# Norms of a two-layer decoder trunk: x turned by products with a diagonal of 1/rms, the upper half of h made by ScalarE from PSUM, lower halves three row blocks later

## The reference

```python
def _rms_norm(x, g):
    y = xf * lax.rsqrt(jnp.mean(xf * xf, axis=-1, keepdims=True) + NORM_EPS)
    return (y * g.astype(jnp.float32)).astype(x.dtype)

def _modulated_norm(x, g, shift, scale):
    return _rms_norm(x, g) * (1.0 + scale[:, None, :]) + shift[:, None, :]

def reference(...):
    for l in range(DEPTH):
        mod = (c_act @ ada_w[l] + ada_b[l]).reshape(bsz, 3, 3, D_MODEL)
        h = _modulated_norm(x, norm_g[l, 0], mod[:, 0, 0], mod[:, 0, 1])
        x = x + MACARON_WEIGHT * mod[:, 0, 2][:, None, :] * _swiglu(h, ffn1_w_in[l], ffn1_w_out[l])
        h = _modulated_norm(x, norm_g[l, 1], mod[:, 1, 0], mod[:, 1, 1])
        mix = _token_mixer(h, positions, mix_w_in[l], ...)
        x = x + mod[:, 1, 2][:, None, :] * mix
        h = _modulated_norm(x, norm_g[l, 2], mod[:, 2, 0], mod[:, 2, 1])
        x = x + MACARON_WEIGHT * mod[:, 2, 2][:, None, :] * _swiglu(h, ffn2_w_in[l], ffn2_w_out[l])
    return _rms_norm(x, final_norm_g)
```

## Time and profile before

| | |
|---|---|
| median of 3 runs | 1481.54 us (1480.98 to 1484.12) |
| the profiled execution's own time | 1479.83 us |
| its span, first to last instruction | 1478.0 us |
| mean granted TensorE clock | 0.985 |
| TensorE busy | 1363.7 us, 92% |
| VectorE busy | 1003.5 us, 68% |
| ScalarE busy | 642.7 us, 43% |
| GpSimd busy | 212.0 us, 14% |
| from HBM | 299.28 MB, 203 GB/s over the span |

### The profile page before, as it was taken

One profiled execution on the slowest core, in us unless ns is written; L12 is line 12 of the kernel. 1 busy time (PEld: TensorE's weight loads), 2 busy tenths in 40 slices (PEclk: granted clock), 3 DMA queues, 4 the chain that ended last, 5 costly groups with the idle time before them and its releaser, 6 DMA issues.

```text
span 1478.0 us, 28648 instructions
## 1 busy us (share of the span) xinstructions
PE 1363.7 (92%) x11945; PEld 1262.1 (85%) x11945; DVE 1003.5 (68%) x1321; ACT 642.7 (43%) x941; POOL 212.0 (14%) x250
## 2 busy tenths in 40 slices
PE   1799998998899998999989999999988999899997
PEld 1799987978689888999879998798867898799986
DVE  5777767657655776776677676775765478766756
ACT  2434335475623335334353343447563343643333
POOL 2032201011020001232003221000102000022200
PEclk9999999999999999999999999999999999999999
DMA  8999976927203857898669996863550095699852
GB/s 291 307 279 270 300 236 194 256 58 194 64 3 101 272 179 209 250 271 269 231 202 273 274 294 245 274 176 96 149 144 10 3 305 180 180 285 261 282 201 100
DMA packets 354073, 301.81 MB, mean 204 GB/s; under 512 B 19871, under 2 KB 295344, under 8 KB 353968
## 3 DMA queue, kind: packets, MB, share of 16 engines
q1 hardware_dynamic: 353968, 300.36, 67.8%
HBM read 299.28 MB, written 1.05 MB: 203 GB/s over the span
## 4 chain that ended last, share of the span: by engine, by line
PE 78%; DVE 12%; ACT 5%; DVEq 2%; issue 1%; DMA 1%; ACTq 0%; SPq 0%
PE PS L1526 17%; PE PS L1474 16%; PE PS L1476 15%; PE PS L1475 15%; DVE wl L933 3%; DVE ada_acc L1021 3%; PE PS L1908 2%; ACT wh L607 2%; PE PS L1556 2%; DVE x L980 1%; DMA raw<-in_mix_w_in 1%; PE PS L1727 1%; PE PS L1563 1%; PE PS L1899 1%; PE PS L1516 1%
## 5 line engine op out<-in xcount | busy, mean ns | idle before, releaser
L933 DVE TENSOR_TENSOR wl<-raw,wh 128x1024 fp32r<-128x1024 f32 (+1 forms) x400 | 468.6, 1212 | 251.7 <-ACT wh L607 251.7
L607 ACT ACTIVATE wh<-raw 128x1024 fp32r<-128x1024 f32 (+1 forms) x400 | 396.7, 1038 | 550.0 <-PE PS L1476 382.1
L1474 PE MATMUL PS<-h_hi,wh 128*128 128x256 f32 x2128 | 606.3, 285 | 18.1 <-DVE h_lo L955 14.1
L1475 PE MATMUL PS<-h_lo,wh 128*128 128x256 f32 x2128 | 598.2, 281 | 0.0
L1476 PE MATMUL PS<-h_hi,wl 128*128 128x256 f32 x2128 | 597.9, 281 | 0.0
L1474 PEld LDWEIGHTS PS<-h_hi,wh 128*128 128x128 f32 x2128 | 406.5, 191 | 23.2 <-issue 20.7
L1475 PEld LDWEIGHTS PS<-h_lo,wh 128*128 128x128 f32 x2128 | 407.9, 192 | 0.6 <-issue 0.5
L1476 PEld LDWEIGHTS PS<-h_hi,wl 128*128 128x128 f32 x2128 | 406.1, 191 | 0.0
L1021 DVE SCALAR_TENSOR_TENSOR ada_acc<-ada_w_ring,cact,ada_acc 128x512 f32<-128x512 f32 x280 | 218.3, 780 | 23.4 <-issue 0.4
L1387 POOL CAST hid_hi<-hf 128x256 fp32r<-128x256 f32 x88 | 64.0, 728 | 434.7 <-DVE hf L992 434.7
L1526 PE MATMUL PS<-wh,hid_hi 128*128 128x512 f32 x320 | 101.4, 398 | 0.0
(11 more groups left out here) (305 smaller groups left out, 1510.6 us busy)
## 6 DMA issues: line engine op xcount, KB each, us to landing
raw<-in_ffn_w_in SPq DMA_DIRECT2D x176, 512.0 KB, 5.4
ada_w_ring<-in_ada_w SPq DMA_DIRECT2D x160, 512.0 KB, 5.1
raw<-in_mix_w_in SPq DMA_DIRECT2D x90, 512.0 KB, 6.2
raw<-in_ffn_w_out SPq DMA_DIRECT2D x44, 1024.0 KB, 5.6
raw<-in_branch_w SPq DMA_DIRECT2D x8, 1024.0 KB, 8.4
raw<-in_mix_w_out SPq DMA_DIRECT2D x8, 1024.0 KB, 4.8
gate_row<-in_ada_b SPq DMA_DIRECT2D x6, 512.0 KB, 6.7
raw<-in_mix_w_in SPq DMA_DIRECT2D x2, 1024.0 KB, 6.3
```

The lines of the kernel that those rows point to most:

```text
L607: nc.scalar.activation(wh[:, s % 2, h * n:(h + 1) * n], raw[:, s % 4, h * n:(h + 1) * n], ACT.Copy).then_inc(*one("w_hi"))
L933: V.tensor_tensor(wl[:, s % 2, h * n:(h + 1) * n], raw[:, s % 4, h * n:(h + 1) * n], wh[:, s % 2, h * n:(h + 1) * n].bitcast(F32), ALU.sub ...
L1474: M(out, wh[(slice(None),) + wsl], rhs_h, start=start, stop=False, skip_group_check=True)
L1475: M(out, wh[(slice(None),) + wsl], rhs_l, start=False, stop=False, skip_group_check=True)
```

## The change

The reciprocal is no longer spread over the partitions. For each half t of the tokens VectorE makes a 128x128 diagonal matrix of 1/rms (`diag_rms`), and TensorE turns x by an fp32 product with it in place of the transpose: turning and scaling in one. The products for half t wait for that half's diagonal, where the transposes waited only for x. ScalarE then makes hh for a row block straight from PSUM, with gsc as its scale and the shift as its bias. VectorE makes scr (now with the shift in it) and hl behind ScalarE, two row blocks at a time. In `first_slot` the wh·hh products of block k are issued first, and wh·hl and wl·hh of block k-3 after them. The split between the first two evacuated groups moves behind the last group, between the two diagonals, and the head of layer 1 (four small VectorE operations) moves ahead of the evacuation that ends layer 0.

```diff
-            def norm_root(l, n, inc=one):
-                dve.wait_ge(*at("rt_ready", 2 * n + 2, l))
-                V.reciprocal(stat[:, 8:10], stat[:, 6:8]).then_inc(*inc("rinv_ready"))
+            def norm_root(l, n, t, inc=one):
+                dve.wait_ge(*at("rt_ready", 2 * n + t + 1, l))
+                V.reciprocal(stat[:, 8 + t:9 + t], stat[:, 6 + t:7 + t])
+                dve.drain()
+                V.tensor_scalar(diag_rms[:, t, :], ident, stat[:, 8 + t:9 + t], None, ALU.mult)\
+                    .then_inc(*inc("diag_ready"))
...
             def norm(l, n):
-                dve.wait_ge(*at("rb_done", n + 1, l))
-                V.tensor_copy(rms, rms_bank(n))
-                dve.drain()
...
                 def lo(c):
-                    dve.wait_ge(*at("hh_ready", n * KD + c + 1, l))
-                    sh = 2 * n * KD + c
-                    V.scalar_tensor_tensor(hl[:, c, :], scr[:, c, :], mod[:, sh:sh + 1],
-                                           hh[:, c, :].bitcast(F32), ALU.add, ALU.subtract)\
+                    dve.wait_ge(*at("t_ready", n * KD + c + 1, l))
+                    V.tensor_tensor(hl[:, c, :], scr[:, c, :], hh[:, c, :].bitcast(F32), ALU.subtract)\
                         .then_inc(*one("h_ready"))
-                for c in range(KD + 2):
...
+                for c in range(0, KD, 2):
+                    dve.wait_ge(*at("hh_ready", n * KD + c + 2, l))
+                    for i in range(2):
+                        sh = 2 * n * KD + c + i
+                        V.tensor_scalar(scr[:, c + i, :], turned(c + i), gsc[:, n, c + i:c + i + 1],
+                                        mod[:, sh:sh + 1], ALU.mult, ALU.add).then_inc(*one("t_ready"))
+                    lo(c)
+                    lo(c + 1)
@@ evac_out
                     if g == 0:
                         ins.then_inc(*one("y_scaled"))
-                        if ls < DEPTH:
-                            split_half(s, 0, still, ls)
                         continue
...
                 if ls < DEPTH:
+                    norm_root(l, n + 1, 0)
+                    split_half(s, 0, still, ls)
+                    norm_root(l, n + 1, 1)
                     split_half(s, 1, still, ls)
@@ ScalarE
-                    nc.scalar.activation(hh[:, c, :], scr[:, c, :], ACT.Identity,
+                    act.wait_ge(*at("x_turned", 4 * n + c // 2 + 1, l))
+                    nc.scalar.activation(hh[:, c, :], turned(c), ACT.Identity, scale=gsc[:, n, c:c + 1],
                                          bias=mod[:, sh:sh + 1]).then_inc(*one("hh_ready"))
@@ TensorE
                 for t in range(TT):
+                    pe.wait_ge(*at("diag_ready", 2 * n + t + 1, l))
+                    for c in range(KD):
+                        ins = M(turned(c)[:, t * P:(t + 1) * P], x[:, t, c * P:(c + 1) * P], diag_rms[:, t, :],
+                                start=c % 2 == 0 and t == 0, stop=True, skip_group_check=True)
+                        if t and c % 2:
+                            ins.then_inc(*inc("x_turned"))
@@ first_slot
+                for k in range(KD + 3):
+                    if k < KD:
+                        pe.wait_ge(*at("w_hi", 2 * s + 2, l))
+                        pe.wait_ge(*at("hh_ready", h0 + k + 1, l))
...
+                    if k < 3:
+                        continue
+                    split_ready(s, 1, still, l)
+                    pe.wait_ge(*at("h_ready", h0 + k - 2, l))
```

More of the change, by code:

```diff
@@ L1060, in _ @@
                 mod_part(l, 0, 16, 4)
-                scales(0)
+                scales(0).then_inc(*one("mod_first"))
+            for l in range(DEPTH):
+                if l == 0:
+                    layer_head(0)
                 if l == 0:
                     split(0, still, l)
-                norm_root(l, 0, one if l else once)
+                dve.drain()
+                if l == 0:
+                    norm_root(0, 0, 0, once)
+                    norm_root(0, 0, 1, once)
                 norm(l, 0)
@@ L1363, in _ @@
                 evac_out(l, 2, 0, l + 1)
-            norm_root(DEPTH, 0)
+            for t in range(TT):
+                dve.wait_ge(*at("rt_ready", t + 1, DEPTH))
+                V.reciprocal(stat[:, 8 + t:9 + t], stat[:, 6 + t:7 + t])
             dve.wait_ge(sem("final_loaded"), 16)
```

44 lines of the change are left out of this document (16 added, 28 removed).

## The result

The changed kernel takes 1491.28 us (median of 12 runs, 1486.33 to 1498.59) against 1482.83 for the kernel before (12 runs, 1478.80 to 1490.65). The ratio is 1.0050, with an interval of 1.0033 to 1.0067: **slower by 0.5%, about 7.4 us**, where I had forecast 1479.0 and a range that ended at 1484. The profiled execution of the changed kernel took 1486.33 us (span 1484.5), 6.5 us over that of before. It was the fastest of the twelve, 5.0 under their median, so it shows less of the loss than a middling execution would. Its mean granted clock is 0.991, higher than the 0.985 of before: it lost time although TensorE fell to half clock less often.

A forecast was written before the change was run, and what follows sets the result against it. TensorE was taken as the bound, at half clock after norms, then VectorE. Gains 1.16 + 0.95 + 2.59 less 0.10, 0.34 and 1.7 made 2.6 us: 1481.54 to 1479.0, range 1474 to 1484.

The forecast's parts named there:

- TensorE at half clock is the late end before: Norm 2, layer 0, kernel before: half clock sets the first slot's end; VectorE's 16 passes end 3.0 us earlier.
- The evacuation and the diagonals: Norm 2, layer 0: moving the split brings x 0.69 us sooner; TensorE's work before h ends 1.3 us later.
- VectorE's passes: Row blocks at a norm: 0.43 us per scalar pass from PSUM, 1.52 a pair; VectorE ends 0.45 us later than before.
- I expect no fall: Five later norms: TensorE's gap of 2.0 us, then unbroken products, leaves the granted clock at 2.4 GHz.
- a later fall: First slot after a norm: if the clock fell there all the same, it costs at most 0.4 us.
- rival 2: Clock falls during the products with the diagonal: first hh 2.05 us later, 7.8 us lost in all, 1489.3; 8%.
- the lever I made of it: Norms: if the clock falls because transposes don't count as busy TensorE, products with the diagonal cure it.
- The first norm: Layer 0's start: products at half clock are not hidden as transposes were; second slot 1.7 us later.
- Rivals 1: VectorE's scalar passes run from PSUM at the SBUF pace of 0.295: 1.1 us less a norm, 1473.6; 7%.
- Rival 3: FFN slots after the norms redrawn to the slow pace: 18 x 0.21 = 3.8 us, 1482.8; 12%.
- Rival 4: VectorE's subtractions wait for its own scalar pass: 0.7 to 1.4 us a norm, 1483 to 1486; 8%.
- Rival 5: The dip in the clock stays, only shifted: at most 0.4 us a norm, 1481; 5%.

The follow-up runs named there:

- b2_old_fill: Kernel before plus two idle fp32 products by TensorE behind the spread of the reciprocal at every norm but the first: 1476.84 us, ratio 0.9968.
- e1_early: Changed kernel with the first norm's diagonals and products made early, among the first sums: 1485.84 us, ratio 1.0018.
- e2_half: Changed kernel with the second mixer slot starting when the first half of its weights is split: 1487.29 us, ratio 1.0033.
- e6_fill: Changed kernel plus two idle fp32 products by TensorE ahead of the products with the diagonal, at the later norms: 1484.43 us, ratio 1.0013.
- e5_back: Changed kernel with the first half's split back between the first two evacuated groups and both diagonals after the last add: 1497.28 us, ratio 1.0104.
- the edits at the mixer norm and at the split's place: Changed kernel, in separate runs: mixer norm in its old form, 1484.23 us, ratio 0.9995; split back between the first two groups, 1497.28 us, ratio 1.0104.
- the other three edits: On the changed kernel: early first norm, second mixer slot by halves, two scr passes on ScalarE; without idle products 1474.28 us, with them 1470.66.
- e12_nofill: Changed kernel with early first norm, second mixer slot by halves and two scr passes on ScalarE, no idle products: 1474.28 us, ratio 0.9948.
- e10_all: Changed kernel with early first norm, second mixer slot by halves, two scr passes on ScalarE and idle products: 1470.66 us, ratio 0.9930.

## Why the prediction failed, step by step

- **TensorE at half clock is the late end before: right at the FFN norms, and it cost more than my sum used.** With no fall the old form gains 1.2 at each norm 2 and 2.1 between the layers, and at most 0.5 at a mixer norm (b2_old_fill). So at the mixer the fall was nearly hidden behind VectorE and had little to give, and what the norm between the layers and norm 2 could gain needed no new form.
- **The evacuation and the diagonals: right.** Last add at G + 4.89, first diagonal done at 6.02 (6.05), second at 7.60 (7.66), the products 3.84 us long to G + 9.9 with the drain.
- **VectorE's passes: the right side, slightly short.** Pair 1.58 against 1.52, so the scalar pass from PSUM has a pace of 0.455 (0.91 for two, 571.40 to 572.31), near the end of 0.48 and far from 0.295. The Trainium skill (VectorE: DVE Perf Modes, "Why PSUM operands drop a tier") holds an fp32 pass with an operand in PSUM to one element a cycle; the trace agrees with it, by this 0.455. VectorE starts at 9.67 (9.58) and ends at 15.97 (15.66). The second slot of an FFN follows at 17.34 (16.93), of the mixer at 18.37 (18.12): 0.4 and 0.25 short at each of five norms, together 1.7 us.
- **"I expect no fall": wrong, the main step.** I rested it on one gap of 2.45 us with the clock at 1.00 in the window that holds its end, and priced a later fall at 0.4 at most, since I put it in the first slot. It fell at three of the five norms, in the products with the diagonal (5.47 us in place of 3.84, my rival 2, which I gave 8%) or in the second slot, which TensorE does at its own pace. That cost 1.6 and 1.8 us at the mixer norms and 1.4 to 1.7 between the layers (-0.3 against the -1.7 to -1.9 of e1_early, e2_half and e6_fill), together 4.9 of the 9.1 us that the profiles lie apart from the forecast. The norm between the layers came to -0.3 against -2.6 forecast, the mixer norms to +1.9 and +2.6 against +0.1 and +0.3. The gap that I took was one of eight: inside the mixers of the kernel before TensorE stands still for 2.4 to 3.1 us eight times, and four of these gaps end in a fall. This is one that I passed over, the row of TensorE and the window behind it, in the columns of the earlier trace rows:

```profile
309.62 1.22 PE L1670 MATMUL PS<-sb_s,cst 128*128 128x256 f32 x2 [2.40 <-DVE sb_s L1096]
...
310.00:311.00 1.00, 1.00 (x4) 0.82 (x4) 1.00 (x2) 1.00 (x2) 0.00 (x0) 0.50 0.00 0
```

  And the gap of the earlier trace rows itself, as long in the changed kernel, ended in a fall there:

```profile
541.99 0.71 PE L1547 MATMUL PS<-wh,h_hi 128*128 128x512 f32 x2 [2.45 <-DVE h_lo L1336]
...
543.00:544.00 1.00, 1.00 (x4) 0.71 (x4) 0.30 (x2) 0.70 (x2) 0.00 (x0) 0.50 0.97 273
```

  So one gap without a fall said next to nothing, and the trace of before was enough to see it.
- **How often it falls at a norm.** Over all profiles of the new form without idle products, 16 of 38 later norms have a fall, with idle products none of 15; in the old form 7 of 7 without and 1 of 10 with them. In the new form it isn't spread evenly: 12 of the 14 mixer norms, 3 of the 8 between the layers, 1 of the 16 norms 2. The gap ahead of the products is 2.0 us in all of them but those of e5_back, where it is 2.7 to 2.9; the one fall at a norm 2 is there. The Trainium skill's sentence that transposes do not count as a busy TensorE (TensorE: Matmul & The Clock Gate, "Part 4: PE-mode transpose") isn't contradicted, but b2_old_fill kept its transposes and lost its falls, so it was not the lever I made of it.
- **The first norm: right mechanism, undersized.** Forecast 1.7; the second slot starts at 62.06 in place of 59.33, 2.7 us, of which 0.3 is a later start of everything. First hh came at 53.34 (52.6) and VectorE added 0.3 as at the other norms. The second slot itself took 0.4 more, which makes the 3.1 of the table, and the three slots behind it ran at 5.65 us in place of 5.44. I saw that these products lose their cover, and took the loss as given; it was the largest single one, and the cheapest to undo.
- **Rivals 1 and 4** (the SBUF pace; a wait of VectorE for itself) didn't occur. **Rival 3** (pace) is real but small: FFN1 of layer 0 lost 0.8 behind the norm's second slot, FFN2 of layer 0 gained 1.0. Rival 4's sum was off as it stood: 0.7 to 1.4 at six norms is 4 to 8 us, not 4 to 7. **Rival 5** (the dip only shifted, at most 0.4 a norm) came true at the mixer norm of layer 0 in its place, into the second slot, and not in its price. **Rival 2** had 1489.3, near the measured 1491.28, but by another sum: it let the clock fall at all five norms for 2.05 us each, and it fell in these products at two, for 1.6. That the numbers are close is luck.
- Profiled against profiled I had 1477.2 and it was 1486.33, 9.1 too low: the norms 8.7 of it (+6.1 against -2.6), of which the first norm 1.4, the mixer norms 4.1, between 2.3, norm 2 0.9. By the medians it was 12.3 too low: I started from 1481.54, the median of three runs where twelve give 1482.83, and added 1.7 from the profiled execution to the median where the changed kernel has 5.0.

What stays open: why the same gap of 2.0 us ends in a fall at nearly every mixer norm and at no norm 2; and why the edits at the mixer norm and at the split's place moved the median by more than their norms show. The falls inside the mixers are the likely carrier of that, but only one execution of each kernel is profiled.

## What to carry to other kernels

When work is moved from an engine with slack to the engine that is the bound (x turned by real products instead of transposes), look for each place where its cover is gone, and for the place where it could run early: here running them early was worth 6 us in the profile. Where two engines end a stage nearly together, taking away what one of them waits for is worth only the distance to the other; measure that distance at each stage, since the mixer norm and the norm ahead of an FFN differed by one wait of 1.1 us. And a gap of TensorE has a price beyond its length: fill it with idle products before you redesign what stands around it, since that test costs two lines and tells how much of the stage was clock. Before you forecast that a clock holds through a gap, list every gap of that length in the trace and count; one that held is no evidence.

## What the runs showed of the hardware

- TensorE's clock after a gap, in 14 profiles: inside the mixers it fell to 0.50 behind 0 of 80 gaps of 1.27 to 1.62 us, 52 of 92 of 2.35 to 2.87 us and 28 of 28 of 2.98 to 3.10 us. At the norms of the new form it fell behind the gap of 2.0 us in 11 of 33 cases (and twice in the second mixer slot, behind the 1.33 us there), behind that of 2.7 to 2.9 us of e5_back in 3 of 5; at those of the kernel before, with 2.4 us, in 5 of 5.
- With two idle fp32 products (1.88 us together) in the gap of 2.0 us no fall stood at any of 15 norms in the new form (16 of 38 without), and at 1 of 10 in the old one (7 of 7 without). The kernels with them are 5.5 us (changed) and 4.7 us (before) faster, with 3.6 and 3.0 of uncertainty; beside the other three edits it is 2.7, not clear of noise. In e6_fill they delay nothing: the first product behind them still waited 0.27 us for its diagonal at each of the five norms.
- A fall at a norm or in a mixer lasted 3.4 us in nearly all cases, or twice that. It cost 1.6 to 1.8 us where TensorE is the bound, 1.7 in the mixers, 1.0 to 1.1 in the products with the diagonal and the first slot of e12_nofill (against e10_all at the mixer norms), and at most 0.5 where VectorE is the bound (before against b2_old_fill at the mixer norms).
- ScalarE makes a 128x256 f32 pass with scale and bias from PSUM in 0.45 us a pass beside VectorE's passes on the same banks, where VectorE takes 0.455.
